# Last key tile of each attention block as one native fp32 value product, one low part moved from GpSimd to VectorE

## The reference, cut to what matters

```python
def _attend(q, k, v):
    s = jnp.einsum('btkgd,bskd->bkgts', q, k).astype(jnp.float32) * (HEAD_DIM ** -0.5)
    p = jax.nn.softmax(s, axis=-1).astype(v.dtype)
    return jnp.einsum('bkgts,bskd->btkgd', p, v)
...
x = x + gt * ((o_lat * jax.nn.silu(gate[:, n_ctx:])) @ w_out)
return _rms_norm(x, final_g)
```

## Time and profile before

| | |
|---|---|
| median of 3 executions | 1234.39 us (1232.46 to 1241.41) |
| the profiled execution, its own time | 1241.58 us |
| its span on the core | 1239.7 us |
| mean granted TensorE clock | 0.989 of full speed |
| busy: PE, DVE, ACT, POOL | 1169.1, 833.8, 514.9, 459.0 us |
| attention, first score matmul to the first output product | 816.3 to 1137.1 us |

### The profile page before, as it was taken

One profiled execution on the slowest core, in us unless ns is written; L12 is line 12 of the kernel. 1 busy time (PEld: TensorE's weight loads), 2 busy tenths in 40 slices (PEclk: granted clock), 3 DMA queues, 4 the chain that ended last, 5 costly groups with the idle time before them and its releaser, 6 DMA issues.

```text
span 1239.7 us, 16979 instructions
## 1 busy us (share of the span) xinstructions
PE 1169.1 (94%) x6594; PEld 956.1 (77%) x6594; DVE 833.8 (67%) x1276; ACT 514.9 (42%) x950; POOL 459.0 (37%) x345
## 2 busy tenths in 40 slices
PE   3899899999999999999999999989999999997997
PEld 2677788887888957878888888867777777776885
DVE  5699829899915254047739785368889898884227
ACT  3445455210015331144425341356766666664012
POOL 4700000000000002433112211169999999997232
PEclk9999999999999999999999999999999999998999
DMA  9935766435422962213021022220000000001303
GB/s 341 343 111 159 184 192 223 141 116 185 160 95 75 329 262 56 68 68 136 1 68 48 22 85 85 78 93 10 18 9 18 9 18 16 12 18 34 137 34 135
DMA packets 81023, 129.83 MB, mean 105 GB/s; under 512 B 12944, under 2 KB 43024, under 8 KB 80144
## 3 DMA queue, kind: packets, MB, share of 16 engines
q1 hardware_dynamic: 71120, 113.96, 27.4%
q10 hardware_dynamic: 9824, 14.80, 3.4%
HBM read 97.81 MB, written 30.93 MB: 104 GB/s over the span
## 4 chain that ended last, share of the span: by engine, by line
PE 59%; POOL 15%; DVE 11%; issue 8%; DMA 5%; ACT 1%; SPq 0%; ACTq 0%; POOLq 0%; DVEq 0%
POOL region_c L689 13%; PE ps L1836 9%; PE ps L1838 9%; PE ps L1837 9%; PE ps L1847 5%; PE ps L1848 5%; PE ps L1849 5%; DVE region_d L1091 3%; PE ps L2190 2%; PE ps L2192 2%; PE ps L2191 2%; PE ps L1996 2%; PE ps L1713 2%; DMA weight_ring<-in_w_mod 1%; POOL ot_lo L679 1%
## 5 line engine op out<-in xcount | busy, mean ns | idle before, releaser
L667 POOL TENSOR_TENSOR region_b<-region_b,region_d 128x512 f32<-128x512 f32 x20 | 26.3, 1329 | 481.1 <-DVE region_d L1486 481.1
L1836 PE MATMUL ps<-w_hi,a_hi 128*128 128x512 f32 x448 | 177.1, 395 | 5.0 <-DVE b_lo L1179 4.4
L1837 PE MATMUL ps<-w_lo,a_hi 128*128 128x512 f32 x448 | 175.1, 391 | 0.0
L1838 PE MATMUL ps<-w_hi,c_lo 128*128 128x512 f32 x368 | 143.3, 389 | 0.0
L1847 PE MATMUL ps<-a_hi,w_hi 128*128 128x512 f32 (+1 forms) x384 | 138.5, 361 | 0.0
L1848 PE MATMUL ps<-b_lo,w_hi 128*128 128x512 f32 (+1 forms) x384 | 136.5, 355 | 0.0
L1849 PE MATMUL ps<-a_hi,w_lo 128*128 128x512 f32 (+1 forms) x384 | 136.3, 355 | 0.0
L1580 DVE TENSOR_REDUCE small<-ps 128x1 f32<-128x1280 f32 x64 | 95.0, 1485 | 54.6 <-PE ps L2118 54.6
L689 POOL TENSOR_TENSOR region_c<-region_c 128x512 f32<-128x512 f32 x80 | 123.4, 1543 | 14.9 <-ACT region_c L1061 10.2
L660 POOL TENSOR_TENSOR w_lo<-weight_ring,w_hi 128x2048 fp32r<-128x2048 f32 x13 | 60.5, 4654 | 184.1 <-ACT w_hi L716 184.1
L1836 PEld LDWEIGHTS ps<-w_hi,a_hi 128*128 128x128 f32 x448 | 84.6, 189 | 24.4 <-issue 6.4
(11 more groups left out here) (242 smaller groups left out, 2711.1 us busy)
## 6 DMA issues: line engine op xcount, KB each, us to landing
weight_ring<-in_w_mod SPq DMA_DIRECT2D x10, 2048.0 KB, 9.3
weight_ring<-in_we_in SPq DMA_DIRECT2D x10, 1024.0 KB, 5.8
weight_ring<-in_wo_in SPq DMA_DIRECT2D x10, 1024.0 KB, 5.1
weight_ring<-cop_t_scratch SPq DMA_DIRECT2D x4, 1536.0 KB, 8.2
region_c<-in_w_mod SPq DMA_DIRECT2D x2, 2048.0 KB, 20.7
bop_scratch<-region_d ACTq DMA_DIRECT2D x16, 256.0 KB, 2.9
cop_t_scratch<-region_d SPq DMA_DIRECT2D x8, 512.0 KB, 7.5
weight_ring<-bop_scratch SPq DMA_DIRECT2D x2, 2048.0 KB, 10.4
```

Of the source, the lines that this page charges most:

```text
L1836: te.matmul(o, th, wh[:, k % 4], start=k == 0, stop=False)
L1837: te.matmul(o, th, wl[:, k % 4], start=False, stop=False)
L1838: last = te.matmul(o, tl, wh[:, k % 4], start=False, stop=k == KT - 1)
```

## The change

- Tile 9 of each block is `plain`: ACT makes no high part of it, nobody a low part, and its value product is one native fp32 matmul of the unsplit `Vt` and `PF` in place of three. It waits only for the exponentials. `Vt`'s tile 9 is left out of the split of the values, since the low part would overwrite it.
- `on_pool` goes from (1, 3, 5) to (1, 4). DVE makes the low parts of tiles 0, 2, 3, 5, 6, 7, 8: still seven. POOL makes two in place of three.
- `KDh` moves from slot 1 of the ring to `shared`, columns 1024 to 3072. So all slots are free for weights: `out1` 0, 1 and 2 are loaded ahead of the attention; `out1` 1 is split ahead of it (ACT after gate piece 14, POOL for the low part) and no longer in the last block. `final_g`, which lay in `shared`, is loaded when the last scores are done.

```diff
-KD_SLOT = 1
...
-        shared = sb("shared", 3072)
+        shared, KDh = region("shared", 3072, [("kd_hi", 1024, 2048)])
...
-        slots = [i for _, i in early] + [i % NSLOT for i in range(len(late) - 4)] + [2, 0, KD_SLOT, 2]
+        slots = [i for _, i in early] + [i % NSLOT for i in range(len(late))]
...
-        on_pool = (1, 3, 5)
+        plain, on_pool = (9,), (1, 4)
+
+        def upto(tiles, m):
+            return len(tiles) * (m // TT) + sum(t <= m % TT for t in tiles)
+
+        def p_done(m):
+            return s_a_ph, m + 1 - upto(plain, m)
...
+        def split_tiles(half):
+            ts = [t for t in range(5 * half, 5 * half + 5) if t not in plain]
...
-                if j in (3, 11, 15):
-                    ring_load(*{3: ("gate", 3), 11: ("out1", 0), 15: ("out1", 1)}[j])
+                if j % 4 == 3:
+                    ring_load(*uses[uses.index(("gate", 3)) + j // 4])
...
-                if i == 0:
-                    sp.wait_ge(s_q_ok, 2 * LT)
-                    sp.wait_ge(s_gt_ev, 6)
-                    sp.dma_start(fgb, final_g.rearrange("(o f) -> o f", o=1).broadcast_to([P, D])).then_inc(s_ld_gain, 16)
             sp.wait_ge(s_a_s, TT * 2 * LT)
-            ring_load("out1", 2)
+            sp.dma_start(fgb, final_g.rearrange("(o f) -> o f", o=1).broadcast_to([P, D])).then_inc(s_ld_gain, 16)
...
-            for u in splits[splits.index(("kv", 1)):splits.index(("out1", 0)) + 1]:
+            for u in splits[splits.index(("kv", 1)):splits.index(("out1", 1)) + 1]:
                 weights_rest(u)
...
+                if j == 14:
+                    weights_round(("out1", 1))
...
                 if m >= NP:
                     i3, t3 = divmod(m - NP, TT)
-                    act.wait_ge(s_a_ph, m - NP + 1)
-                    act.wait_ge(*p_rest_done(m - NP))
+                    if t3 not in plain:
+                        act.wait_ge(*p_done(m - NP))
+                        act.wait_ge(*p_rest_done(m - NP))
                     act.wait_ge(s_a_sum, 9 * i3 + max(t3, 1))
                 a.activation(PF[m % NP], ps[:, 3 + m % 2, :], ACT.Exp).then_inc(s_a_p, 1)
-                act.wait_ge(s_a_p, m + 1)
-                copy(p_hi[:, m % NP], PF[m % NP]).then_inc(s_a_ph, 1)
+                if t not in plain:
+                    act.wait_ge(s_a_p, m + 1)
+                    copy(p_hi[:, m % NP], PF[m % NP]).then_inc(s_a_ph, 1)
...
-                if m == TT * 2 * LT - 7:
-                    weights_round(("out1", 1))
...
-                if m and (m - 1) % TT not in on_pool:
-                    dve.wait_ge(s_a_ph, m)
+                if m and (m - 1) % TT not in on_pool + plain:
+                    dve.wait_ge(*p_done(m - 1))
...
-                if m == TT * 2 * LT - 5:
-                    dve.wait_ge(s_w_lo, splits.index(("out1", 1)))
-                    weights_rest(("out1", 1))
...
-                te.matmul(o, Vh[:, t, hd], p_hi[:, m % NP], start=t == 0, stop=False)
-                te.matmul(o, Vh[:, t, hd], p_lo[:, m % NP], start=False, stop=False)
-                mm = te.matmul(o, Vl[:, t, hd], p_hi[:, m % NP], start=False, stop=t == TT - 1)
+                if t in plain:
+                    mm = te.matmul(o, Vt[:, t, hd], PF[m % NP], start=t == 0, stop=t == TT - 1)
+                else:
+                    te.matmul(o, Vh[:, t, hd], p_hi[:, m % NP], start=t == 0, stop=False)
+                    te.matmul(o, Vh[:, t, hd], p_lo[:, m % NP], start=False, stop=False)
+                    mm = te.matmul(o, Vl[:, t, hd], p_hi[:, m % NP], start=False, stop=t == TT - 1)
```

More of the change, by code:

```diff
@@ L158, in build @@
         KTh, KTl = (q.rearrange("p (j t) -> p j t", t=TOK) for q in (KTh, KTl))
-        KDh = w_split[2 * KD_SLOT + 1].rearrange("p (j t) -> p j t", t=TOK - 2 * P)
+        KDh = KDh.rearrange("p (j t) -> p j t", t=TOK - 2 * P)
         BL = [RC[:, 2048 * i:2048 * i + 2048].rearrange("p (r g s h) -> p r g s h", r=2, g=8, h=HC) for i in range(2)]
@@ L375, in x1_done @@
             return s_o_ok, TT + t + 1
-        on_pool = (1, 3, 5)
-        def p_rest_done(m):
-            n = len(on_pool) * (m // TT) + sum(t <= m % TT for t in on_pool)
-            return (s_a_plp, n) if m % TT in on_pool else (s_a_pld, m + 1 - n)
+        plain, on_pool = (9,), (1, 4)
[3 more added lines that the diff above has]
+            return s_a_ph, m + 1 - upto(plain, m)
+        def p_rest_done(m):
+            n = upto(on_pool, m)
+            return (s_a_plp, n) if m % TT in on_pool else (s_a_pld, m + 1 - upto(plain, m) - n)
+        def split_tiles(half):
+            ts = [t for t in range(5 * half, 5 * half + 5) if t not in plain]
+            assert ts == list(range(ts[0], ts[-1] + 1))
+            return slice(ts[0], ts[-1] + 1)
         def y_sem(fb):
@@ L691, in _ @@
                 if t in on_pool:
-                    pool.wait_ge(s_a_ph, m + 1)
+                    pool.wait_ge(*p_done(m))
                     g.tensor_tensor(p_lo[:, m % NP], PF[m % NP], p_hi[:, m % NP].bitcast(F32), ALU.subtract).then_inc(s_a_plp, 1)
@@ L1030, in _ @@
                 if j == 9:
-                    act.wait_ge(s_g_mm, 8)
                     act.wait_ge(s_kt_lo, 10)
@@ L1036, in _ @@
                     q_round(j - 10)
+                if j == 14:
+                    weights_round(("out1", 1))
             act.wait_ge(s_g_mm, 2 * NH)
             def values_round(kv, half):
-                ts, hd = slice(5 * half, 5 * half + 5), slice(HD * kv, HD * kv + HD)
+                ts, hd = split_tiles(half), slice(HD * kv, HD * kv + HD)
                 copy(Vh[:, ts, hd], Vt[:, ts, hd]).then_inc(s_v_hi, 1)
@@ L2152, in values @@
                 i, t = divmod(m, TT)
-                pe.wait_ge(*p_rest_done(m))
+                if t in plain:
+                    pe.wait_ge(s_a_p, m + 1)
+                else:
+                    pe.wait_ge(*p_rest_done(m))
                 if t in (0, 5) and i < 2:
```

## The result

The changed kernel takes 1223.19 us (median, 1223.00 to 1223.38) against 1237.66 for the kernel before beside it: the ratio is 0.9886, 95% interval 0.9841 to 0.9931. The forecast was 1216.9, its range 1209 to 1231; the time lies within that and 1.2 above the forecast's own narrower range, 1212 to 1222. The profiled execution took 1223.03, of which the span is 1221.2; before it was 1239.7, so the sum to be explained is 18.5 us, of which the prediction gave 17.5.

What follows compares the result with a forecast made beforehand. POOL was taken as the bound, PE about 1 us behind. Blocks 3 to 14 gave 8.9 us and block 15 8.6, together 17.5, so 1216.9 against the median of 1234.39; the range was 1209 to 1231.

Steps and rivals of the forecast that it cites:

- the forecast's own narrower range: Whole kernel: 1212 to 1222, from bounds of blocks 0 and 1, the native matmul and the tie in some blocks.
- The blocks: Blocks 3 to 14: each goes from 19.84 to 19.1 us, 8.9 us in all; block 2 gives 0.
- The tie: Each block's end: DVE's low part 7 gets in at a POOL addition's start, taking 0.68 us, as in block 2.
- The rival of the lost tie: Each block's end: low part 7 waits, 0.94 us more, 20.04 a block; -5.3 us, 1229; chance 0.15.
- Block 15: Last attention block: 5.7 us of waits and 2.9 of slow clock go, less slow-start and native-product costs; 8.6 us together.
- Blocks 0 and 1: First two blocks, 40.77 us together before: no change expected, with 1.5 us either way.
- a sign of being wrong: Blocks 0 and 1: growing by more than 1.5 us would show the prediction wrong.
- The native product: Tile 9 on PE: one fp32 matmul of 0.86 us replaces three of 0.69 together, 0.17 more work a block.
- Only PE bounds: Rival, 13 blocks: low part 6 doesn't wait, PE runs at 18.75; 4.5 us more gain, 1212.4; chance 0.12.
- PE is the bound and the stall moves: Rival: the 1.02 us stall only changes name, a block costs 0.17 more; 1228.4; chance 0.08.
- block 15 gives nothing: Rival, block 15: another wait or the clock takes its place; -8.9 us, 1225.5; chance 0.10.
- DVE's list in tiles 5 to 8: Rival: low parts wait for whole POOL instructions, row maximum 3 starts later; 20.6 us a block, 1236.4; chance 0.07.

Runs made afterwards that it cites:

- the control: The changed kernel run again, unchanged: 1220.51 us, ratio 0.9873 to the kernel before.
- tile 5 on POOL: Against the changed kernel, POOL makes low parts 1 and 5 in place of 1 and 4: 1221.61 us, ratio 0.9873 to the kernel before.
- the values late: Against the changed kernel, the low parts of the second head's values go behind the first block's `neg_max` on DVE: 1222.00 us, ratio 0.9874.
- `neg_max` first: Against the changed kernel, `neg_max` goes ahead of low part 7, behind `output`, in tile 8: 1221.55 us, ratio 0.9884 to the kernel before.
- the nudge: Against the changed kernel, a one-column memset on DVE between `output` and low part 7: 1237.10 us, ratio 0.9994 to the kernel before.
- `neg_max` first with the nudge: Against the changed kernel, `neg_max` ahead of low part 7 and a one-column DVE memset behind `output`: 1220.02 us, ratio 0.9876 to the kernel before.
- the weights alone: Against the kernel before, only the moved weights and `KDh`; all ten tiles split, POOL makes low parts 1, 3, 5: 1233.08 us, ratio 0.9974.

## Why the prediction was right

**The blocks.** 8.9 us were forecast for blocks 3 to 14, 9.9 came. A block takes 18.92, not 19.1: PE's wait for `neg_max`, with its slow start, is shorter than I took it for, 18.92 - 18.65 = 0.3. Block 10, with 20.06, costs 1.1 of it. DVE idles 0.46 ahead of `output`, POOL's addition gets in first (1025.28 against 1025.64), and low part 7 takes 1.48:

```profile
1025.03 0.69 DVE L1613 TENSOR_TENSOR region_d<-region_c,ps 128x512 f32<-128x512 f32 x1 [0.46 <-DVE region_c L1603]
1025.28 1.28 POOL L695 TENSOR_TENSOR region_c<-region_c,region_b 128x512 f32<-128x512 f32 x1
1025.64 1.48 DVE L1641 TENSOR_TENSOR p_lo<-region_c,p_hi 128x512 fp32r<-128x512 f32 x1
```

It stands in the same block in the control, with tile 5 on POOL, and with the values late, so it is no chance. The same 0.46 also stands in block 10 with `neg_max` first (1021.75), where it costs nothing: only with low part 7 on the path does it lose the tie. What makes DVE idle there is open.

**The tie** was the step on which most hung, and it was read from one block of the old trace. That it came out as there was partly luck: nothing in the prediction could tell which way a start within 0.01 us falls, and it said so with 0.15 for the other way. Two readings around it were off without harm. Low part 6 does not end together with a POOL instruction: in the two blocks read it ends 0.55 after one (873.48 in block 2, 1051.14 in block 11). And the reason given for the tie coming back, no low part 5 on POOL, was too narrow, as above. The nudge, and `neg_max` first with the nudge, show it. The rival of the lost tie had its block right (20.04, measured 20.07) but not its sum: -5.3 us forecast, -3.2 in the stretch (423.4 to 420.2), since it left out blocks 0 and 1, 1.1 longer with the nudge, and took 8.6 for block 15 where 8.0 came. Its times then can't be told from those of the kernel before.

**Block 15.** 8.6 forecast, 5.9 + 1.9 = 7.8 measured; by the weights alone 5.3 of it. The slow clock before lay on both sides of the first matmul of `out1` (1137.11), where the count of block 15 ends:

```profile
1135.28 0.63 PE L2147 MATMUL ps<-q_t_lo,w_hi 128*128 128x512 f32 x1
1135.70 0.63 PE L2148 MATMUL ps<-q_t_hi,k_t_lo 128*128 128x512 f32 x1
1137.11 0.77 PE L1836 MATMUL ps<-w_hi,ot_hi_a 128*128 128x512 f32 x1 [0.78 <-ACT region_b L1061]
```

Matmuls 0.43 apart in place of 0.23 cost about 0.7 in block 15 and 2.1 behind it, so nearly all of the 2.9 came back, and part of it is in the 5.9. Most of what is missing of the 8.6 is in the waits: PE still waits 0.3 for POOL there, and the first matmul of `out1` waits 1.1 for the last exponentials, where it waited 0.8 before. The weights themselves cost nothing ahead of the attention, as forecast: POOL's low part of `out1` 1 took 4.62 (6.2 was the estimate), and POOL still idled 3.78 before its first addition.

**Blocks 0 and 1.** 0 with 1.5 either way; the profiled run gives +1.6, the control -0.1. Growth of more than 1.5 was named as a sign of being wrong; it came in the first profile, and the control shows that it was the clock and not DVE's list. Block 0 is 1.5 longer (20.26 to 21.81): PE waits 1.4 for a row maximum and 2.5 for `neg_max` behind DVE's full list, where it had waited 1.7 for POOL and 0.2 for `neg_max`. Block 1 is 1.6 shorter (20.51 to 18.91 in the control), since a wait of 1.3 for DVE's row maximum is gone; where the clock falls it takes that back. So 0 was the balance of two terms of 1.5 that the prediction had not seen, and in that it was lucky. I had not thought of the clock here.

**The native product** costs 0.86, as its rows said. By the Trainium skill's four passes ("FP8 and Floating Point Precision", section "TensorE Precision Notes") it would be dearer than three fp32r matmuls of 0.23, and it is, by 0.17. It still pays: it takes a low part from DVE and a rounding from ACT, and with it alone, beside the weights, a block is 0.34 shorter (19.80 to 19.46).

**The rivals.** "Only PE bounds" (18.75) fell for the change; it needed `neg_max` first, and then it holds, at 18.65. "PE is the bound and the stall moves" and "block 15 gives nothing" fell. DVE's list in tiles 5 to 8 did not grow; with 20.6 a block it would have.

The median missed by 6.3 us. Of that 3.3 is the base: the sum was made against 1234.39, and the kernel before took 1237.66 beside the change. The difference was 14.5 instead of 17.5; the profiled executions, with 16.3 in the attention and behind it, and the control, with 16.7 between the medians, lie between. Within the 16.3, blocks 2 to 14 gave 1.2 more than the 8.9 forecast, even with block 10; blocks 0 and 1 came out short by 1.6 (the clock) and block 15 by 0.8 (mostly the waits). Finer than this the runs don't tell.

## What to carry to other kernels

A stall that is removed is worth what the next engine's path lets through, so follow that path instruction by instruction in a block where the stall happens to be missing: one such block of the old trace gave 19.1 and the change 18.92. Where two engines exclude each other and meet at an equal time, a 0.06 us instruction can cost 15 us; don't tune such a tie, move the instruction that has slack out of the path. And when you move an instruction later, look at who reads it and what stands behind that reader in its queue.

## What the runs showed of the hardware

A low part on DVE (two inputs from SBUF) and POOL's additions and low parts exclude each other for the whole of an instruction in the timelines shown: 0.68 and 1.83 when DVE is first, 1.82 and 1.48 when POOL is. DVE's row maximum, `gate_over_sums` and `output`, with an input in PSUM, took 1.48 or 1.49, 0.67 or 0.68, and 0.69 beside POOL in every block of the traces before and after. PE's clock was at 0.50 for some microseconds after waits of 1.4 and 2.5 us in three traces and stayed at 1.00 after the same waits in four others. And two engines that start within 0.01 us of each other kept the same order in the same 13 blocks of three traces (the change, the control, tile 5 on POOL), and lost it in all 14 with a memset of 0.06 us put in.
